# A two-block transformer kernel: position tiles as a row of the compressing layer's moving tiles, its parameters loaded during the first FFN, key zeros by VectorE, and new orders in both attentions, the FFN and the decay series

## The chip, the cores and the metric

One core of one Trainium2 chip runs the whole program. The metric is device time in microseconds (us) from the start to the end of the launch, as a median of runs. The profile is one execution of the same program.

## The reference

All is fp32 with D = 1024 features, 256 tokens and batch 1. A first block has two layers; in each, the normalized input goes through one wide projection and feeds a gated spatial unit, a latent attention with 8 heads (MLA) and a linear recurrence, whose outputs are projected, gated and merged. A second block has a pooling mixer, a convolutional FFN (FFN 0), a sparse attention (NSA) with compressed keys and values, and a second FFN (FFN 1); behind each FFN stands a gated addition ("ple"). The parts that the change touches:

```
def rg_lru(...):                      # first block, per layer
    log_a = -LRU_C * r * softplus(-lam)        # the "decay" of each of 1280 channels
    a = exp(log_a) ...
def compress(blocks, pos_emb, w1, w2):         # 15 blocks of 32 tokens, 4 groups, for keys and for values
    z = blocks + pos_emb
    z = z.reshape(z.shape[:3] + (CMP_LEN * HEAD_DIM,))
    return jax.nn.gelu(z @ w1) @ w2            # 2048 -> 128 -> 64
def conv_ffn(h, w_up, conv_w, conv_b, w_down): # 1024 -> 2 x 2816 -> 1024
def nsa_attention(...): # 16 heads; softmax over the compressed blocks, over the selected and over the windowed keys, gated
```

## The kernel before, in words

The program is raw per-engine code with semaphores; every engine's order is written out by hand. SP issues the weight loads, POOL (GpSimd) issues the small ones and does some memsets. **Weights** stream as pieces of at most 512 KB through a ring of six raw buffers (`load`): SP issues the load of a piece once PE has begun the piece five before. ACT rounds each piece to `w_hi` (L1244, `hi`), DVE computes `w_lo = raw - w_hi` (L1771, `lo`), and PE adds three products for each fp32 product (L601, L604, L605: hi by hi, lo by hi, hi by lo). In the ACT and DVE programs `hi(j, half)` and `lo(j, half)` stand where these engines make the pieces of slot j ahead, so the order of those calls among the other work decides when PE gets a piece. PSUM banks are taken in turn from two rings: J (banks 0 to 3) for projections, K (4 to 7) for side jobs.

**A norm** before a projection: ACT squares x (L1262) and takes the root (L1290), DVE the reciprocal (L1783) and a diagonal matrix (L1789), and PE multiplies x by it, which turns and scales x in one step (L724, `turn_x`, 32 matmuls, 16 for each token tile); ACT and DVE then split it into `h_hi` (L1300, `split_h`) and `h_lo` (L1805, `low_h`). Because Sqrt, Exp and the like need different tables, ACT loads a table ahead with `preload` (L1284).

**First layer's decays**: a series of 32 in-order DVE operations on 128x20 tiles (`decay_series`, `decay_terms`, `decay_result`, L1854 to L1870), placed behind `lo(0, ...)` and ahead of the convolution (L1931) in steps i = 1 to 3 of the recurrence's input projection (`l == 0` only).

**MLA**: the last gate tiles `zb` are evicted by ACT (L1249) after `hi(1, 1)`, and then come `turned` (evictions p0T, p1T of the transposed probabilities), which PE waits for at L858.

**Compressing layer**: `constant_term` (L1003 to L1009) computes w1 transposed times the position embedding as 16 matmuls of one column for the values (before `turn_x` of the ple of FFN 0) and 16 for the keys (job "bias" before `turn_x` of the key/value projection); DVE copies each to `pb` (L2348) and adds it to the hidden layer's bank. `hidden` does 2 x 16 matmuls with 60 moving columns (4 groups x 15 blocks) out of `cc`. w1 (two 1 MB loads, L576), w2, the positions and the memsets of w2 and vcz are issued by POOL in the pooling mixer's stage, just before FFN 0; POOL zeroes all of `kz` (4096 elements a partition, L580) during `turn_x` of the key/value projection.

**NSA attention**: `NSA_JOBS` is the order of the jobs on ring K: S (scores, L1097 to L1107), X (transposes of the exponentials, L1126), V (values, L1140), C (combination, L1151), "cs" (compressed scores, L1202), ct (transposes of the compressed weights Tc). ACT takes the exponentials (L1712) with the maxima that DVE makes (L2499), and evicts transposes as t0T, t1T and tcT (L1249).

## Time and profile before

| what | value |
|---|---|
| runs | 1531.07, 1532.56, 1538.85 us (median 1532.56) |
| profiled execution | 1533.47 us |
| its span in the profile | 1531.4 us |
| mean granted TensorE clock | 0.986 of full |
| DMA | 240.99 MB, mean 157 GB/s |

All times of places below are us from the start of the profiled span. A timeline row gives start, duration (of a group: from its first start to its last end), engine, line, operation, and in brackets how long the engine had been idle before and what ended that.

### The profile page before, as it was taken

The page shows a single profiled execution, that of the slowest core. Times are in us where ns is not written, and L with a number is a line of the kernel's source. Part 1 is how long each engine was busy: PE and PEld are TensorE (multiplying, and loading weights), DVE is VectorE, ACT ScalarE, POOL GpSimd, SP SyncE. Part 2 cuts the span into 40 slices and gives each one's busy share as a digit, 9 for nine tenths or more (in the row PEclk, how much of TensorE's full clock was granted, in tenths as well). Part 3 has the DMA queues.
Part 4 walks back from the last instruction along what each step waited for, and adds up shares of the span by engine and source line. Part 5 has one row for each costly group of instructions (what it writes and reads, how often), then busy time and mean ns, then how long its engine had stood idle before and what let it go on. Part 6 is the DMA issues. An engine that isn't in the chain of part 4 may idle for free.

```text
span 1531.4 us, 23284 instructions
## 1 busy us (share of the span) xinstructions
PE 1476.0 (96%) x9421; PEld 1338.5 (87%) x9421; DVE 1047.6 (68%) x1571; ACT 873.2 (57%) x1512; POOL 87.1 (6%) x137
## 2 busy tenths in 40 slices
PE   8899999999999999999999899999999989999997
PEld 7898989788789889997888799988899778999886
DVE  6645669986666366698967678864566644788745
ACT  6465756564454657565645566653674543766545
POOL 9000000007000000000000100000000000000000
PEclk9999999999999999999999999999999989999999
DMA  8524376566556144765675555556435003655553
GB/s 240 160 75 145 111 217 182 179 190 195 187 155 173 50 145 120 226 190 171 190 226 179 157 171 187 180 166 188 129 99 154 28 1 110 193 180 185 180 172 110
DMA packets 188890, 240.99 MB, mean 157 GB/s; under 512 B 19022, under 2 KB 133890, under 8 KB 188784
## 3 DMA queue, kind: packets, MB, share of 16 engines
q1 hardware_dynamic: 182944, 228.66, 49.7%
q0 software_dynamic: 5744, 10.82, 2.4%
q8 instruction: 75, 1.23, 0.3%
q14 instruction: 31, 0.25, 0.1%
q10 hardware_dynamic: 96, 0.03, 0.0%
HBM read 238.42 MB, written 1.05 MB: 156 GB/s over the span
## 4 chain that ended last, share of the span: by engine, by line
PE 84%; DVE 6%; ACT 6%; DMA 2%; issue 1%; SPq 0%; DVEq 0%; ACTq 0%
PE bank L601 24%; PE bank L605 24%; PE bank L604 24%; PE bank L724 2%; PE bank L797 2%; DVE w_lo L1771 2%; PE bank L1140 2%; ACT w_hi L1244 1%; ACT T L1712 1%; DMA raw<-in_ffn_up 1%; PE bank L1126 1%; DMA raw<-in_mla_w_ukv 1%; ACT S L1421 1%; PE bank L735 1%; DMA raw<-in_w_out 0%
## 5 line engine op out<-in xcount | busy, mean ns | idle before, releaser
L1771 DVE TENSOR_TENSOR w_lo<-raw,w_hi 128x1024 fp32r<-128x1024 f32 (+2 forms) x452 | 521.3, 1171 | 271.3 <-ACT w_hi L1244 269.1
L1244 ACT CAST w_hi<-raw 128x1024 fp32r<-128x1024 f32 (+2 forms) x452 | 450.5, 1007 | 292.6 <-DMA raw<-in_w_in 118.4
L601 PE MATMUL bank<-h_hi,w_hi 128*128 128x256 f32 (+1 forms) x1640 | 465.7, 284 | 6.2 <-issue 4.1
L604 PE MATMUL bank<-h_lo,w_hi 128*128 128x256 f32 (+1 forms) x1640 | 463.6, 283 | 0.0
L605 PE MATMUL bank<-h_hi,w_lo 128*128 128x256 f32 (+1 forms) x1640 | 463.6, 283 | 0.0
L601 PEld LDWEIGHTS bank<-h_hi,w_hi 128*128 128x128 f32 (+1 forms) x1640 | 312.9, 191 | 7.2 <-issue 7.0
L604 PEld LDWEIGHTS bank<-h_lo,w_hi 128*128 128x128 f32 (+1 forms) x1640 | 313.0, 191 | 0.1
L605 PEld LDWEIGHTS bank<-h_hi,w_lo 128*128 128x128 f32 (+1 forms) x1640 | 313.0, 191 | 0.0
L601 PE MATMUL bank<-w_hi,h_hi 128*128 128x512 f32 (+1 forms) x464 | 176.9, 381 | 1.1 <-issue 1.1
L605 PE MATMUL bank<-w_hi,h_lo 128*128 128x512 f32 (+1 forms) x464 | 175.6, 378 | 0.0
L604 PE MATMUL bank<-w_lo,h_hi 128*128 128x512 f32 (+1 forms) x464 | 175.5, 378 | 0.0
L601 PEld LDWEIGHTS bank<-w_hi,h_hi 128*128 128x128 f32 x464 | 87.3, 188 | 18.2 <-issue 2.3
L605 PEld LDWEIGHTS bank<-w_hi,h_lo 128*128 128x128 f32 x464 | 87.3, 188 | 16.5
L604 PEld LDWEIGHTS bank<-w_lo,h_hi 128*128 128x128 f32 x464 | 87.3, 188 | 15.9
L601 PE MATMUL bank<-w_hi,y_hi 128*128 128x512 f32 x176 | 69.8, 397 | 2.0 <-DVE w_lo L1771 2.0
L604 PE MATMUL bank<-w_lo,y_hi 128*128 128x512 f32 x176 | 69.6, 396 | 0.0
L605 PE MATMUL bank<-w_hi,y_lo 128*128 128x512 f32 x176 | 69.6, 395 | 0.0
L724 PE MATMUL bank<-diag,x 128*128 128x128 f32 x256 | 40.7, 331 | 10.7 <-DVE diag L1789 9.9
L724 PEld LDWEIGHTS bank<-diag,x 128*128 128x128 f32 x256 | 39.3, 243 | 12.4 <-DVE diag L1789 10.9
L1257 ACT ACTIVATE ug<-bank,par 128x256 f32<-128x256 f32 x44 | 24.9, 566 | 43.9 <-PE bank L605 43.9
L797 PE MATMUL bank<-xc,wg 128*128 128x256 f32 x208 | 45.8, 380 | 1.2 <-ACT R L1390 1.2
L797 PEld LDWEIGHTS bank<-xc,wg 128*128 128x128 f32 x208 | 39.2, 190 | 7.4 <-ACT R L1390 2.0
(356 smaller groups left out, 2150.6 us busy)
## 6 DMA issues: line engine op xcount, KB each, us to landing
raw<-in_w_in SPq DMA_DIRECT2D x160, 512.0 KB, 3.8
raw<-in_ffn_up SPq DMA_DIRECT2D x88, 512.0 KB, 3.6
raw<-in_ffn_down SPq DMA_DIRECT2D x40, 512.0 KB, 4.5
raw<-in_w_proj_a SPq DMA_DIRECT2D x16, 512.0 KB, 3.6
raw<-in_w_proj_b SPq DMA_DIRECT2D x16, 512.0 KB, 3.6
raw<-in_w_proj_c SPq DMA_DIRECT2D x16, 512.0 KB, 3.7
raw<-in_w_out SPq DMA_DIRECT2D x16, 512.0 KB, 3.7
raw<-in_ple_gate SPq DMA_DIRECT2D x16, 512.0 KB, 4.2
```

Source lines behind the costliest of these rows:

```text
L601: first = pe.matmul(out_, lh, rh, start=start, stop=False)
L604: pe.matmul(out_, lh, rl, start=False, stop=False)
L605: return pe.matmul(out_, ll, rh, start=False, stop=stop)
L724: mm = pe.matmul(ps[b][:, at:at + P], x[:, t, k * P:(k + 1) * P], diag[:, t, :], start=True, stop=True)
L735: mm = pe.transpose(ps[b][:, n * P:(n + 1) * P], src, c["ident"])
L797: mm = pe.matmul(acc(b), wg[:, g, rep, pair, :], xc[:, 5 * rep + i_, :], start=(n == 0), stop=(n == len(near) - 1))
L1126: mm = pe.transpose(ps[b][:, n * P:(n + 1) * P], src, c["ident"])
L1140: mm = pe.matmul(o_, pt, vsw[:, k, a, g * HD:(g + 1) * HD], start=k == 0, stop=k == qt)
L1244: act.copy(w_hi[b][:, 0:size], raw[b][:, 0:size]).then_inc(sems["hi_done"], 1)
L1257: act.activation(dst, acc(b), func, bias=bias, scale=scale)\
L1421: ins_ = act.activation(S[:, hd, :], S[:, hd, :], ACT.Exp, bias=sm[:, 1, col + hd:col + hd + 1], accum_out=sm[:, 2, col + hd:col + hd + 1])
L1771: dve.tensor_tensor(w_lo[b][:, 0:size], raw[b][:, 0:size], w_hi[b][:, 0:size].bitcast(F32), ALU.subtract).then_inc(sems["w_split"], 1)
```

## The change

1. `cc` gets a ninth row of 256 columns, shared by the keys' and the values' half, which holds the position embeddings at the columns that the strided view reads; the hidden layer's matmuls move 75 columns in place of 60, and both `constant_term` and their copies are gone; DVE copies the two constants out of the hidden bank with one more copy (128x2).
2. The positions and w1 are loaded in the up part of FFN 0, w1 in four quarters of 512 KB, each released by a step of it; w2 and the two memsets come behind its last step.
3. The zeros of `kz` are set by DVE, only the halves that need them, as two memsets 64x2048 in the ple of FFN 0.
4. In NSA attention the transposes of Tc go behind X1 on PE, their evictions behind t1T/t0T of head group 1 on ACT; DVE makes four `w_lo` pieces ahead of the Tc chain; ACT loads the Sqrt table behind the last t1T/t0T.
5. In both MLA layers the last zb eviction and the last `hi`/`lo` of that slot stand behind the first `turned` or the y tiles.
6. In both FFNs ACT's Sqrt table load goes from ahead of the down projection's pieces to behind those of its first half.
7. At the key/value projection ACT makes two more pieces ahead of four copies to m (`keep`).
8. The decay operations stand ahead of `lo(0, ...)`, in steps 2 to 4.
9. At the start SP issues the first weight slot before it waits for x.

```diff
-NSA_JOBS = (["bias"] + [f"norm{u}" for u in range(KT // 2)] + ["hidden", "keys0", ...]
+NSA_JOBS = ([f"norm{u}" for u in range(KT // 2)] + ["hidden", "keys0", ...]
-            + [f"X0.{i}" for i in range(6)] + ["swap3", "V0.1", "V0.0", "cs", "ct0", "ct1"]
-            + [f"X1.{i}" for i in range(6)] + ["V1.1", "V1.0", "C0"]
+            + [f"X0.{i}" for i in range(6)] + ["swap3", "V0.1", "V0.0", "cs"]
+            + [f"X1.{i}" for i in range(6)] + ["ct0", "ct1", "V1.1", "V1.0", "C0"]
...
-            sp.wait_ge(sems["x_in1"], 16)
...
                     load(0, rows_of(w_in, l, 0, KT, i * SW + COL_XC, SW))
+                    if (l, i) == (0, 0):
+                        sp.wait_ge(sems["x_in1"], 16)
...
-            pool.wait_ge(sems["sq_part"], 4 + 8 * L)
+            pool.wait_ge(sems["f_ready"], 2 + 2)
...
+            for n, key in enumerate(("cmp_w1_k_2", "cmp_w1_v_2")):
+                for half in range(2):
+                    pool.wait_ge(sems["f_ready"], 2 + 4 * (2 * n + half + 1))
+                    pool.dma_start(w1[:, n, 8 * half:8 * half + 8, :],
...
+            pool.wait_ge(sems["f_ready"], 2 + FT)
...
-            pool.wait_ge(sems["sq_part"], 4 + 8 * L + 12)
-            pool.memset(kz[:, :, :, :, :], 0.0).then_inc(sems["nsa_zero"], w.given("nsa_zero"))
...
-                if l == 0:
-                    pe.wait_ge(sems["nsa_in"], 96)
-                    filled(constant_term(side(), 1), w.bank("K"))
                 turn_x()
...
-            filled(constant_term(b, 0), b)
...
-                    mm = pe.matmul(ps[b][:, 64 * n:64 * n + 60]..., w1[:, n, k, :],
-                                   cc[:, n, :, 2 * k:2 * k + 225:16], ...)
+                    mm = pe.matmul(ps[b][:, 75 * n:75 * n + 75]..., w1[:, n, k, :],
+                                   cc[:, 4 * n:4 * n + 5, 2 * k:2 * k + 225:16], ...)
...
             scores2(2)
+            turn2(1)
             pe.wait_ge(sems["tc_done"], 1)
             for i in range(2):
                 transposes_at(job(f"ct{i}"), ...)
-            turn2(1)
...
                 if keep:
+                    keep()
...
-                        hi(j, n)
-                        evac("J", 2 * j + n, zb[:, dyn(i, 4, 2 * j + n), :], ACT.Silu)
+                        if (i, j, n) != (1, 1, 1):
+                            hi(j, n)
+                            evac("J", 2 * j + n, zb[:, dyn(i, 4, 2 * j + n), :], ACT.Silu)
...
                 turned(1, 1)
+                evac("J", -1, zb[:, HEADS - 1:HEADS, :], ACT.Silu)
...
                     y_tile(8 + n, 4 + n, yb_hi)
+                hi(-1, 1)
...
-                preload(ACT.Sqrt)
                 for n in range(2):
                     for j in range(5 if n else 6):
                         hi(j, 0), hi(j, 1)
+                    if n == 0:
+                        preload(ACT.Sqrt)
...
+            def second_slot():
+                hi(-1, 0), hi(-1, 1)
+            split_h(lambda k: col(ROW2["kv"] + k), keep=second_slot)
...
                         lo(1, 0), lo(1, 1)
+                        if l == 0:
+                            position_terms()
+                            clear_keys()
...
+            def position_terms():
+                dve.memset(cc[:, NG, :], 0.0).then_inc(sems["dve_step"], w.given("dve_step"))
+                dve.wait_ge(sems["dve_step"], w.value("dve_step"))
+                for n, key in enumerate(("posk", "posv")):
+                    dve.tensor_copy(cc[:, NG, 32 * n:32 * n + 32:2], col(ROW2[key], 16)).then_inc(sems["pos_set"], 1)
+            def clear_keys():
+                dve.memset(kz[64:P, 0, :, :, :], 0.0)
+                dve.memset(kz[0:64, 1, :, :, :], 0.0)
```

The order of DVE's instructions in the first layer's recurrence projection before, step 1 (xc is the convolution, dt the decays; ahead stand the pieces `lo(0, 0)` and `lo(0, 1)`):

```order
L1771 TENSOR_TENSOR w_lo<-raw,w_hi 128x1024 x2
L1854 TENSOR_SCALAR dt<-dt 128x20
L1855 RECIPROCAL dt<-dt 128x20
L1856 TENSOR_TENSOR dt<-dt 128x20
L1857 TENSOR_TENSOR dt<-dt 128x20
L1858 TENSOR_SCALAR dt<-dt 128x20
L1931 SCALAR_TENSOR_TENSOR xc<-bank,par,xc 128x255
```

and of the change, from the end of step 1's convolution into step 2:

```order
L1932 SCALAR_TENSOR_TENSOR xc<-bank,par,xc 128x253
L1770 TENSOR_TENSOR w_lo<-raw,w_hi 128x1024 x2
L1853 TENSOR_SCALAR dt<-dt 128x20
L1854 RECIPROCAL dt<-dt 128x20
L1855 TENSOR_TENSOR dt<-dt 128x20
L1856 TENSOR_TENSOR dt<-dt 128x20
L1857 TENSOR_SCALAR dt<-dt 128x20
L1862 TENSOR_TENSOR dt<-dt 128x20
```

The series moved from ahead of a convolution to behind the convolution and behind `lo(1, 0)` and `lo(1, 1)`; its terms follow there in the same way, four pairs or fewer a step.

DVE in the ple of FFN 0, of the change (before, the two m/x operations follow the w_lo group directly):

```order
L1804 SCALAR_TENSOR_TENSOR h_lo<-bank,par,h_hi 128x256 x8
L1770 TENSOR_TENSOR w_lo<-raw,w_hi 128x1024 x6
L2352 MEMSET cc 128x256
L2355 COPY cc<-par 128x16 x2
L2359 MEMSET kz 64x2048
L2360 MEMSET kz 64x2048
L2340 TENSOR_TENSOR m<-G,m 128x512
L2343 TENSOR_TENSOR x<-x,m 128x512
```

Five operations are added there, ahead of the additions that end in the next norm.

ACT in NSA attention, before, from the exponentials of head group 2 on:

```order
L1712 ACTIVATE T,sums<-bank,nm 128x128 x8
L1249 ACTIVATE tcT<-bank 128x512 x2
L1249 ACTIVATE t1T<-bank 128x512 x2
L1249 ACTIVATE t0T<-bank 128x512
L1724 CAST h_hi<-bank 128x512
```

and of the change:

```order
L1711 ACTIVATE T,sums<-bank,nm 128x128 x8
L1245 ACTIVATE t1T<-bank 128x512 x2
L1245 ACTIVATE t0T<-bank 128x512
L1245 ACTIVATE tcT<-bank 128x512 x2
L1723 CAST h_hi<-bank 128x512
```

The evictions of tcT moved behind those that the transposes of head group 1 fill.

## Rows read from the trace of the kernel before

**Rows 1.** The page's busy times, whole span.
```profile
PE 1476.0 (96%) x9421; PEld 1338.5 (87%) x9421; DVE 1047.6 (68%) x1571; ACT 873.2 (57%) x1512; POOL 87.1 (6%) x137
```
**Rows 2.** PE's waits: who waited for what, total us, times, longest.
```profile
PE bank L724 <- DVE diag L1789: 9.9, 4, 6.2
```
**Rows 3.** Timeline of PE, first layer, three starts of a slot.
```profile
39.13 0.36 PE L601 MATMUL bank<-h_hi,w_hi 128*128 128x256 f32 x1 [0.80 <-issue]
...
52.21 0.35 PE L601 MATMUL bank<-h_hi,w_hi 128*128 128x256 f32 x1 [1.34 <-issue]
...
65.91 0.36 PE L601 MATMUL bank<-h_hi,w_hi 128*128 128x256 f32 x1 [1.96 <-issue]
```
**Rows 4.** Timeline of DVE at the same place.
```profile
43.62 1.22 DVE L1771 TENSOR_TENSOR w_lo<-raw,w_hi 128x1024 fp32r<-128x1024 f32 x1 [2.33 <-ACT w_hi L1244]
...
48.96 0.18 DVE L1864 TENSOR_SCALAR dt<-dt 128x20 f32<-128x20 f32 x1
...
59.40 1.22 DVE L1771 TENSOR_TENSOR w_lo<-raw,w_hi 128x1024 fp32r<-128x1024 f32 x1 [3.89 <-ACT w_hi L1244]
```
**Rows 5.** Timeline of PE, MLA of the first layer.
```profile
185.81 0.46 PE L858 MATMUL bank<-p0T,vm 128*128 128x128 f32 x2 [1.38 <-ACT p1T L1249]
```
**Rows 6.** Timeline of PE, pooling mixer to FFN 0.
```profile
875.76 6.26 PE L724 MATMUL bank<-diag,x 128*128 128x128 f32 x32 [6.20 <-DVE diag L1789]
```
**Rows 7.** Timeline of DVE, same place.
```profile
871.67 1.23 DVE L1771 TENSOR_TENSOR w_lo<-raw,w_hi 128x1024 fp32r<-128x1024 f32 x1 [5.68 <-ACT w_hi L1244]
```
**Rows 8.** Timeline of ACT, same place.
```profile
870.60 1.04 ACT L1244 CAST w_hi<-raw 128x1024 fp32r<-128x1024 f32 x1 [8.71 <-DMA raw<-in_ffn_up]
```
**Rows 9.** DMA issues, 850 to 884 us: count, KB each, us to landing.
```profile
w<-in_cmp_w_v POOLq DMA_DIRECT2D x1, 1024.0 KB, 10.7
```
**Rows 10.** DMA issues, 880 to 1003 us, the up part of FFN 0.
```profile
raw<-in_ffn_up SPq DMA_DIRECT2D x39, 512.0 KB, 3.6
```
**Rows 11.** Timeline of PE, down part of FFN 0.
```profile
1018.12 0.50 PE L601 MATMUL bank<-w_hi,y_hi 128*128 128x512 f32 x1 [0.98 <-DVE w_lo L1771]
```
**Rows 12.** Timeline of ACT, same place.
```profile
1014.36 1.28 ACT L1284 ACT_TABLE_LOAD   x1
```
**Rows 13.** Timeline of PE, FFN 0 to its ple.
```profile
1071.42 3.63 PE L1007 MATMUL bank<-par,w 128*128 128x1 f32 x32
...
1080.27 0.47 PE L601 MATMUL bank<-w_hi,h_hi 128*128 128x512 f32 x1
```
**Rows 14.** Timeline of PE, FFN 1 to its ple.
```profile
1497.12 1.95 PE L724 MATMUL bank<-diag,x 128*128 128x128 f32 x16
...
1501.55 0.47 PE L601 MATMUL bank<-w_hi,h_hi 128*128 128x512 f32 x1
```
**Rows 15.** Timeline of PE, ple of FFN 0 to the key/value projection.
```profile
1102.13 3.63 PE L1007 MATMUL bank<-par,w 128*128 128x1 f32 x32
...
1113.06 0.36 PE L601 MATMUL bank<-h_hi,w_hi 128*128 128x256 f32 x1
```
**Rows 16.** Timeline of DVE, same place.
```profile
1105.49 0.16 DVE L1783 RECIPROCAL st<-st 128x1 f32<-128x1 f32 x1 [1.11 <-ACT st L1290]
```
**Rows 17.** DVE's groups by form: count, busy us, mean ns, idle before.
```profile
L2405 DVE MEMSET TcP<- 128x1024 f32 x1 | 0.9, 912 | 0.3 <-DVE sin L2402 0.3
```
**Rows 18.** Timeline of PE, key/value projection, second slot.
```profile
1120.64 0.36 PE L601 MATMUL bank<-h_hi,w_hi 128*128 128x256 f32 x1 [1.59 <-DVE w_lo L1771]
```
**Rows 19.** Timeline of PE, NSA attention.
```profile
1223.90 0.50 PE L1104 MATMUL bank<-causal_r,ident_r 128*128 128x512 f32 x1 [2.74 <-ACT T L1712]
...
1232.17 3.45 PE L1126 MATMUL bank<-cst,T 128*128 128x128 f32 x16 [3.88 <-ACT tcT L1249]
...
1254.68 0.29 PE L1140 MATMUL bank<-vsw,t1T 128*128 128x64 f32 x1 [1.31 <-ACT t1T L1249]
```
**Rows 20.** Stretches: from:to, length, busy PE, PEld, DVE, ACT, POOL, then granted clock, DMA share, GB/s.
```profile
1253.00:1264.00 11.00, 9.69 (x55) 9.48 (x54) 3.12 (x7) 2.02 (x5) 0.00 (x0) 0.65 0.01 2
...
424.00:440.00 16.00, 13.16 (x87) 11.92 (x86) 10.27 (x26) 10.14 (x27) 0.00 (x0) 1.00 0.43 126
```

More of the change, by code:

```diff
@@ L182 @@
     _at += _n
[L185 removed]
+NSA_JOBS = ([f"norm{u}" for u in range(KT // 2)] + ["hidden", "keys0", "keys1", "kc", "vc", "gates", "kc_swap", "swap0", "swap1"]
             + [f"S0.{i}" for i in range(6)] + ["swap2"] + [f"S1.{i}" for i in range(6)]
[L187 to L188 removed]
+            + [f"X0.{i}" for i in range(6)] + ["swap3", "V0.1", "V0.0", "cs"]
+            + [f"X1.{i}" for i in range(6)] + ["ct0", "ct1", "V1.1", "V1.0", "C0"]
             + [f"X2.{i}" for i in range(6)] + ["V2.1", "V2.0"] + [f"X3.{i}" for i in range(6)]
@@ L997, in ffn @@
                 w.go("J", 4)
-                if l == 0:
-                    pe.wait_ge(sems["nsa_in"], 96)
-                    filled(constant_term(side(), 1), w.bank("K"))
                 turn_x()
                 wide_square("ple", h, "h_ready", in_turn=True)
-            def constant_term(b, n):
-                for k in range(16):
-                    mm = pe.matmul(ps[b][:, n:1 + n], w1[:, n, k, :],
-                                   par[:, ROW2["posv" if n else "posk"] + k:ROW2["posv" if n else "posk"] + k + 1],
-                                   start=(k == 0), stop=(k == 15))
-                return mm
             ffn(0)
@@ L1738, in _ @@
             exps2(2)
+            turned2(1)
             for i in range(2):
                 evac("K", at(f"ct{i}"), tcT[:, 2 * i:2 * i + 2, :].rearrange("p a n -> p (a n)"), width=512)
-            turned2(1)
             high_o(0)
             exps2(3)
-            preload(ACT.Sqrt)
             high_o(1)
@@ L1747, in _ @@
             turned2(3)
+            preload(ACT.Sqrt)
             high_o(2)
@@ L1915, in _ @@
                         decay_input()
+                    if l == 0 and i == 2:
+                        decay_series()
+                        decay_terms(15, 13)
+                    if l == 0 and i == 3:
+                        decay_terms(11, 5)
+                    if l == 0 and i == 4:
+                        decay_terms(3, 1)
+                        decay_result()
                     for n in range(2):
@@ L2027, in _ @@
                         for half in range(2):
-                            lo(j, half)
+                            if (col, j, half) != (0, 1, 1):
+                                lo(j, half)
                     w.go("S", 2), w.go("J", 4)
-                for j in range(1, 5):
+                for j in range(2, 5):
                     dve.wait_ge(free[w.bank("J", -j)], w.turn("J", -j) + 1)
@@ L2048, in _ @@
                 for t in range(HEADS):
+                    if t + 1 == HEADS - 1:
+                        dve.wait_ge(free[w.bank("J", -1)], w.turn("J", -1) + 1)
                     if t + 1 < HEADS:
@@ L2562, in _ @@
             weigh2(0)
+            for j in (2, 3):
+                lo(j, 0), lo(j, 1)
             b = w.bank("K", at("cs"))
@@ L2570, in _ @@
                 .then_inc(sems["tc_ready"], 1)
-            for j in (2, 3):
-                lo(j, 0), lo(j, 1)
             w.go("S", 4), w.go("J", 8)
```

67 lines of the change are left out of this document (25 added, 42 removed).

## The prediction, made before the changed kernel was run

> **What bounds the kernel now.** I read the page first: PE is busy for 96% of the span [rows 1], so at most some 55 us are to be had from its idle time, and everything else must come from matmuls removed or from matmuls that run at a faster clock. Then I read PE's waits, in which no single cause is large; the largest is `turn_x` waiting for its diagonal, 9.9 us in four places [rows 2]. So the change can only be a collection of small holes, and I went to the timeline at each place that the diff touches. A hole counts only if the engine named before the arrow does work that the change moves, and if nothing else is ready only then.
>
> **The parts and their sum**, all against the profiled execution (1533.47 us; the median of the runs is 0.9 us lower).
>
> *Decays.* PE starts three slots late, by 0.80, 1.34 and 1.96 us [rows 3], at the steps in which DVE does 5, 8 and 11 decay operations ahead of the convolution. One takes 0.18 us and, with the wait between them, about 0.21. Moved ahead of `lo(0, 0)` they are 9, 8 and 7 operations, 1.9, 1.7 and 1.5 us. DVE stands idle there for 2.33 us in one step and 3.89 us one piece later in the next [rows 4], so they are hidden. Gain 4.1. Without that cover each would cost PE its full length again, and the gain would be 0.
>
> *MLA.* PE waits 1.38 us for the eviction of p1T [rows 5]; ahead of it on ACT stand one rounding of a piece, 1.04 us as at [rows 8], and one eviction, which leave. What is late next is the first eviction itself, so I take 1.1 for each of two layers: 2.2. The moved piece is needed only by a slot that PE reaches behind the attention, and DVE's `lo` of it follows the y tiles.
>
> *Pooling mixer to FFN 0.* DVE waits 5.68 us for a rounded piece [rows 7], because ACT waits 8.71 us for its raw load [rows 8]. At that time 2 MB of w1 are in flight, of which a megabyte took 10.7 us [rows 9]; in the up part of FFN 0 a weight piece lands 3.6 us after its issue [rows 10]. With w1 elsewhere the load is there when DVE comes, and both diagonals are ready 5.7 us earlier. PE's turn then takes 32 x 0.12 = 4 us in place of 6.26 [rows 6, 14], as its idle time shrinks from 6.2 to about 0.5 us and the clock has no reason to fall. 5.7 + 2.0 = 7.7.
>
> *Table load in the down part.* ACT loads the Sqrt table, 1.28 us [rows 12], ahead of six slots' pieces, and PE then idles 0.98 us for a `w_lo` [rows 11]. Behind the six slots ACT is ahead of PE. Two FFNs: 2.0.
>
> *First constant.* From the end of the down part to the first matmul of ple, FFN 0 takes 1080.27 - 1071.42 = 8.85 us [rows 13]; FFN 1, which has no constant, 1501.55 - 1497.12 = 4.43 us [rows 14]. Gain 4.4.
>
> *Second constant and the key zeros.* From 1102.13 to 1113.06 stand 10.93 us [rows 15]. Without the 16 columns and with DVE as now, the second diagonal, some 0.5 us behind the reciprocal at 1105.49 [rows 16], would set the end: 1106 and 2 us of turning for the second token tile, a gain of 5. But DVE gets new work ahead: a memset of 1024 elements takes 0.912 us [rows 17], so two of 2048 take up to 3.6, and with the memset of 256 and two copies 4.3. DVE has 0.5 us to spare there, so the diagonals come near 1105.0 and 1109.7, PE turns one tile, waits, turns the other and goes on at 1111.7. Gain 1.3, between 5 (all covered) and -2 (both waits at half clock).
>
> According to the Trainium skill (VectorE: DVE Perf Modes, Zero memsets can be issued as uint32 (trn2) and Specifications) a memset takes one cycle for an element at 0.96 GHz. That would be an estimate of 2.13 us for each of the two, and of 0.6 us less gain. The trace's 912 ns for 1024 elements is under the 1067 ns of that rule, and the row decides.
>
> *Position columns.* 75 columns in place of 60 cost nothing: matmuls of one column were 3.63 us for 32, 0.11 each [rows 15], which is no less than those of 128 columns [rows 14]. The copy of the constants is one small DVE operation: 0.2 against the removed two. POOL's memset of `kz` goes: 0, nobody waited.
>
> *Two pieces ahead at the key/value projection.* PE waits 1.59 us for a `w_lo` [rows 18]; the rounding comes before four copies of about half a microsecond. Gain 1.6.
>
> *NSA attention.* Three holes [rows 19]. 2.74 us: the exponentials wait for the maxima, which stand behind four `w_lo` pieces on DVE; these go into the time in which DVE waits for "cs". Gain 2.7. 3.88 us: PE's turn of X1 stands behind the transposes of Tc, whose eviction on ACT comes behind sixteen exponentials; X1 now goes first, into other banks, and about 3.0 are won, the rest being the exponentials' own. 1.31 us: the table load stands ahead of t1T: 1.3. Together 7.0.
>
> *w1 in FFN 0.* 2 MB beside a stream that lands well before it is needed: -0.3, between 0 and -4, by what the 2 MB do today in a busier place [rows 8].
>
> *Clock.* Attention runs at half clock in stretches (0.65 at 1253 to 1264), while an idle time of 3 us inside dense work shows none (1.00 at 424 to 440) [rows 20]. With holes closed but narrow matmuls packed closer I take -1, between -4 and +3.
>
> *Start.* The first slot's 1 MB is asked for ahead of x's end. PE is bound there by the small rows and x: 0, between -1 and +0.5.
>
> Sum: 4.1 + 2.2 + 7.7 + 2.0 + 4.4 + 1.3 + 1.6 + 7.0 - 0.3 - 1 = 29.0. The profiled execution would take 1504.5 us, and the median **1503.5 us**.
>
> **The rivals.**
>
> (A) *The zeros cost more than the constants gave.* The two DVE memsets make PE wait twice for about 3 us, and around two narrow, broken turns the clock stays down. The half-clock turn of [rows 6] took 6.26 in place of 4; twice that and a slower first slot are 2 to 4 us. The time would be 1506.5. For it: the stretch is narrow already. Against it: 3 us of idle did not lower the clock at 424 to 440.
> By the Trainium skill (TensorE: Matmul & The Clock Gate, What's actually happening) the slow state is the default and activity lifts it, so broken turns are punished; the trace shows both behaviours.
>
> (B) *Waits move rather than go.* In attention PE, ACT and DVE each depend on the next; a closed hole may open behind the next exponentials, and the same may hold for the decays. If half of the attention's, the decays' and the slot's gains come back, 12.7 / 2 = 6.4 are lost: 1510.
>
> (C) *w1's quarters stop FFN 0.* Each quarter may delay the weight pieces behind it. PE would have to stop for 7.3 us at each of the four to use up 29 us, as ACT did once for 8.71 [rows 8]; at the point from which this decides, 7.5 us and more each, the kernel ends slower than before, at 8.71 each 1503.5 + 34.8 = 1538. Against it: there 2 MB at once and x's norm came together, here 512 KB come over several slots, and the stream lands in 3.6 us.
> The Trainium skill (DMA: Bandwidth & Descriptors, Measured) says to batch DMAs to 1 MiB and more, which speaks against quarters; the weight pieces of half a megabyte show no such need, at 3.6 us each. A milder form, 1 to 2 us a quarter, gives 1508 to 1511.
>
> (D) *The early loads do nothing*, because something other than w1 delayed the piece at 870.6. Then 7.7 go: 1511. Against it: other pieces of the same stream land in 3.6 us.
>
> **How the numbers follow.** Forecast 0.55 (1498 to 1508), A 0.15, B 0.15, a mild C 0.06, D 0.04, strong C 0.02, and 0.03 for more gain (clock restored in attention, zeros covered, 1493 to 1498). The range of 1496 to 1512 holds the forecast, A, B and D, and leaves out strong C and the tails. 0.5% is 7.7 us, about what a measurement of this kernel can tell from no change: everything under 1524.9 counts as faster. Only a strong C or several failures at once end above: faster 0.94, same 0.04, slower 0.02.
>
> **What the profile of the changed kernel would show.** Decays: no late starts near 39, 52 and 66 us. Pooling: the wait for the diagonal falls from 6.2 to under 1.5 us, and ACT's wait for the first FFN piece is gone. Constants: no matmul of one column; ple of FFN 0 begins 4.5 us after its down part. Zeros: two waits for the diagonal of about 2.8 us each before the key/value projection. FFN 0: w1 quarters at steps 2 to 8, and no PE wait on raw pieces beside them. Attention: no wait of over 1.5 us on the maxima, tcT or t1T. It would be wrong if FFN 0 from up to down got longer by over 2 us, if the two diagonal waits together exceeded 8, or if attention shortened by less than 4.

## The result and the profile after

The changed kernel takes 1507.64 us (median of 5 runs, 1501.28 to 1510.37) against 1533.38 us for the kernel before (5 runs, 1531.07 to 1538.85): ratio 0.9826, 95% interval 0.9802 to 0.985. That is 25.7 us between the medians; 1503.5 was forecast, with 1496 to 1512 as the range. The profiled execution happened to be the shortest of the five: 1501.28 us, span 1499.5, mean clock 0.994. The other four took 1507.2 to 1510.4 at clocks of 0.990 and 0.991. So the profile shows 31.9 us of gain and the median 6 less, and what lies between them became the main question.

The busy times on the page of the changed kernel, to be read beside [rows 1]:

```profile
PE 1458.7 (97%) x9357; PEld 1321.4 (88%) x9357; DVE 1048.9 (70%) x1575; ACT 873.6 (58%) x1512; POOL 84.6 (6%) x138
```

and two of PE's waits (total, times, longest), beside [rows 2] and [rows 5]:

```profile
PE bank L730 <- DVE diag L1788: 9.4, 6, 3.8
...
PE bank L864 <- ACT p1T L1245: 0.9, 2, 0.5
```

64 matmul records are gone (9421 to 9357), the two constants. The wait for the diagonals is as large as before in sum, but it has moved: the 6.2 us ahead of FFN 0 are gone, and 3.8 and 1.1 us stand ahead of the key/value projection.

I then laid the starts of the same PE instruction in both profiles side by side. What a stage won is the change of that difference from one row to the next:

| PE instruction | before, us | after, us | difference | this stage |
|---|---|---|---|---|
| end of first turn | 13.83 | 13.71 | -0.12 | start: 0.1 |
| slot behind the last decays | 65.91 | 61.05 | -4.86 | decays: 4.7 |
| first L858 of MLA, layer 1 | 185.81 | 179.67 | -6.14 | MLA: 1.3 |
| product of c, layer 2 | 552.86 | 548.83 | -4.02 | -2.1 (scatter, below) |
| first L858 of MLA, layer 2 | 602.59 | 597.73 | -4.86 | MLA: 0.8 |
| first product of FFN 0 | 881.78 | 869.15 | -12.63 | pooling mixer: 7.8 |
| slot in its down part | 1018.12 | 1004.33 | -13.79 | w1 in FFN 0: 0; table: 1.1 |
| first product of its ple | 1080.27 | 1061.96 | -18.31 | first constant: 4.5 |
| last of the key/value turn | 1112.64 | 1093.81 | -18.83 | second constant, zeros: 0.5 |
| two slots later | 1127.11 | 1105.88 | -21.23 | pieces ahead: 2.4 |
| late in the hidden layer | 1144.83 | 1126.06 | -18.77 | given back: a wait 1.4, columns 1.1 |
| first V1 | 1235.41 | 1210.75 | -24.66 | attention: waits 4.9, clock 1.1 |
| first V2, behind the table load | 1254.68 | 1228.45 | -26.23 | table: 1.3, clock 0.3 |
| X3, behind V2 | 1267.16 | 1236.44 | -30.72 | clock in V2 and X3: 4.5 |
| slot in the down part of FFN 1 | 1443.82 | 1412.02 | -31.80 | table: 1.1 |

The rows of the changed kernel that answer to [rows 3], [rows 5], [rows 6], [rows 11], [rows 13], [rows 15] and [rows 19], PE's timeline (start, duration, instruction, idle before):

```profile
61.05 0.28 PE L607 MATMUL bank<-h_hi,w_hi 128*128 128x256 f32 x1
...
179.67 0.35 PE L864 MATMUL bank<-p0T,vm 128*128 128x128 f32 x1 [0.45 <-ACT p1T L1245]
...
865.06 1.16 PE L730 MATMUL bank<-diag,x 128*128 128x128 f32 x8 [0.43 <-DVE diag L1788]
...
1061.96 0.47 PE L607 MATMUL bank<-w_hi,h_hi 128*128 128x512 f32 x1
...
1087.73 3.40 PE L730 MATMUL bank<-diag,x 128*128 128x128 f32 x16 [3.76 <-DVE diag L1788]
1092.26 2.05 PE L730 MATMUL bank<-diag,x 128*128 128x128 f32 x16 [1.14 <-DVE diag L1788]
1094.15 0.36 PE L607 MATMUL bank<-h_hi,w_hi 128*128 128x256 f32 x1
...
1113.07 0.35 PE L607 MATMUL bank<-h_hi,w_hi 128*128 128x256 f32 x1 [1.21 <-issue]
...
1206.91 1.25 PE L1122 MATMUL bank<-cst,T 128*128 128x128 f32 x8 [0.43 <-DVE t1T L2528]
1209.85 1.07 PE L1122 MATMUL bank<-cst,TcP 128*128 128x128 f32 x8 [1.69 <-ACT t1T L1245]
1210.75 3.68 PE L1136 MATMUL bank<-vsw,t1T 128*128 128x64 f32 x32
1214.27 1.95 PE L1136 MATMUL bank<-vsw,t0T 128*128 128x64 f32 x16
```

Three things are to be seen. The late starts of the decay slots have no idle time any more. A new wait of 1.21 us stands at 1113.07, two slots behind the hole that was closed: ACT is busy without a break there, so part of what the earlier pieces gave comes back. And ahead of V1 there is a new hole of 1.69 us (1209.85): the first transpose of Tc needs a bank that ACT frees only when it evicts X1.2, behind all the exponentials of head group 2. The 4.5 us of clock are those of V2 and of the transposes behind it (X3): the kernel before ran them at half clock [rows 20], this execution at full clock. Another 1.1 us of clock lies ahead of V1: behind the hole of 3.88 us the kernel before took 3.45 us for 16 records of transposes [rows 19], and the two rows of eight here took 1.25 and 1.07. (Counts behind an x are records; a matmul of the constants or of the hidden layer leaves two.)

DVE's timeline at the zeros:

```profile
1075.76 1.76 DVE L2359 MEMSET kz<- 64x2048 f32 x1 [0.48 <-issue]
1077.99 1.76 DVE L2360 MEMSET kz<- 64x2048 f32 x1 [0.46 <-issue]
...
1087.39 0.29 DVE L1788 TENSOR_SCALAR diag<-cst,st 128x128 f32<-128x128 f32 x1
```

From the last `w_lo` of that place to the first m operation lie 5 us, and from there DVE goes on to the diagonal at 1087.4 with one break of 1.1 us, in which ACT takes the root.

### The profile page after: what moved, and what is told of

Read it like the earlier page. It is cut to its first block, busy times and chain, and to the rows that moved or that the text cites. A ratio compares the mean times of both kernels' runs of the same rounds, so it can differ in the third digit from the quotient of the medians.

```text
span 1499.5 us, 23159 instructions
## 1 busy us (share of the span) xinstructions
PE 1458.7 (97%) x9357; PEld 1321.4 (88%) x9357; DVE 1048.9 (70%) x1575; ACT 873.6 (58%) x1512; POOL 84.6 (6%) x138
## 3 DMA queue, kind: packets, MB, share of 16 engines
HBM read 238.42 MB, written 1.05 MB: 160 GB/s over the span
## 4 chain that ended last, share of the span: by engine, by line
PE 87%; DVE 6%; ACT 3%; DMA 2%; issue 2%; POOL 0%; DVEq 0%; POOLq 0%
PE bank L607 25%; PE bank L610 25%; PE bank L611 25%; PE bank L803 2%; DVE w_lo L1770 1%; PE bank L1136 1%; PE bank L730 1%; ACT T L1711 1%; PE bank L741 1%; DMA raw<-in_mla_w_ukv 1%; PE bank L1093 1%; DMA raw<-in_w_out 1%; PE bank L1050 1%; ACT w_hi L1240 1%; PE bank L1122 1%
## 5 line engine op out<-in xcount | busy, mean ns | idle before, releaser
L1599 ACT ACTIVATE sg<-ug 128x256 f32<-128x256 f32 x44 | 18.4, 418 | 46.4 <-DVE ug L2298 46.4
L730 PE MATMUL bank<-diag,x 128*128 128x128 f32 x256 | 36.0, 303 | 9.5 <-DVE diag L1788 9.4
```

Of the source, the lines that this page charges most:

```text
L730: mm = pe.matmul(ps[b][:, at:at + P], x[:, t, k * P:(k + 1) * P], diag[:, t, :], start=True, stop=True)
L1599: act.activation(sg[:, n, :], ug[:, n, :], ACT.Silu)\
```

## The experiments

**The changed kernel once more.** No edit.

> The changed kernel as it is. Its five executions so far took 1501.3 to 1510.4 us, with mean granted clocks of 0.994 (1501.3), 0.991 (1507.2, 1507.6) and 0.990 (1509.6, 1510.4). Theory 1: the difference is one or two stretches that run at half clock in most executions and at full clock in the profiled one; 0.003 to 0.004 of 1500 us are 9 to 12 us at half clock, or 4.5 to 6 us of time. Then a run of 1507 us shows such a stretch, most likely in the narrow matmuls of NSA attention (at 1228 to 1240 us in the profile of the change the clock was 1.00), and differs from the profiled one nowhere else by more than 1 us. Theory 2: the difference lies in waits on DMA spread over the program; then no single stretch holds more than half of it.

Median 1508.07 us (6 runs): 1501.1 and 1501.9 at clock 0.994, and 1508.0, 1508.1, 1508.3, 1512.5 at 0.989 to 0.991. This time the profile is of a run of 1508.02. PE's timeline of it, where the two profiles part:

```profile
1209.97 1.53 PE L1122 MATMUL bank<-cst,TcP 128*128 128x128 f32 x8 [1.69 <-ACT t1T L1245]
1211.29 6.93 PE L1136 MATMUL bank<-vsw,t1T 128*128 128x64 f32 x32
1218.01 3.62 PE L1136 MATMUL bank<-vsw,t0T 128*128 128x64 f32 x16
1221.42 1.17 PE L1144 MATMUL bank<-tcT,vcz 128*128 128x256 f32 x2
```

and the same stretch with its granted clock (third number from the end), from this profile

```profile
1211.20:1224.60 13.40, 13.40 (x63) 13.04 (x62) 2.23 (x4) 0.69 (x2) 0.00 (x0) 0.52 0.01 1
```

and from the shorter one:

```profile
1210.70:1217.50 6.80, 6.80 (x59) 6.70 (x58) 2.23 (x4) 0.95 (x2) 0.00 (x0) 1.00 0.01 2
```

The same 32 matmuls of V1 take 6.93 us in place of 3.68. Up to 1207 us no start differs by more than 0.5 us; from V1 on the difference grows by 0.1 us with each record, to 6.7 us behind the combination, and then stays. Theory 1 holds, with the place 17 us ahead of where I had put it: 1.2 GHz in one execution, 2.4 in the other, behind the same idle time of 1.69 us. The idle time two rows earlier differs a little, 0.78 us in place of 0.43.

**The old orders in NSA attention.** The three moves undone:

```diff
-            turn2(1)
             pe.wait_ge(sems["tc_done"], 1)
             for i in range(2):
                 transposes_at(job(f"ct{i}"), ...)
+            turn2(1)
...
-            turned2(1)
             for i in range(2):
                 evac("K", at(f"ct{i}"), ...)
+            turned2(1)
...
-            for j in (2, 3):
-                lo(j, 0), lo(j, 1)
             b = w.bank("K", at("cs"))
...
                 .then_inc(sems["tc_ready"], 1)
+            for j in (2, 3):
+                lo(j, 0), lo(j, 1)
...
+            preload(ACT.Sqrt)
             high_o(1)
             turned2(2)
             turned2(3)
-            preload(ACT.Sqrt)
```

> The changed kernel with the old orders in NSA attention (transposes of Tc ahead of X1, four w_lo pieces behind the Tc chain, Sqrt table ahead of t1T). If the three holes add: 2.7 + 3.0 + 1.3 = 7.0 us more, median 1514 to 1515, with waits of 2.7, 3.9 and 1.3 us at the old places. If the orders only moved waits: under 4 us more. If they also changed the clock behind them, up to 12 us more, with a half-clock stretch of some 10 us behind the transposes.

Median 1508.67 us (4 runs, 1507.93 to 1514.1): no more than the changed kernel in the same session (1508.07). The holes are all back in PE's timeline:

```profile
1205.52 0.80 PE L1100 MATMUL bank<-causal_r,ident_r 128*128 128x512 f32 x1 [4.45 <-ACT T L1711]
...
1213.80 2.02 PE L1122 MATMUL bank<-cst,T 128*128 128x128 f32 x16 [2.65 <-ACT tcT L1245]
1215.73 3.76 PE L1136 MATMUL bank<-vsw,t1T 128*128 128x64 f32 x32
...
1234.87 1.30 PE L1136 MATMUL bank<-vsw,t1T 128*128 128x64 f32 x10 [1.32 <-ACT t1T L1245]
```

Against the 1501 us profile PE is 1.9 us behind at 1190 us, ahead of the stage, and 6.4 behind at 1235 and at the end, so by place the three undone moves cost 4.6 us. (In between it was 1.5 ahead, because the scores ran at full clock in this execution; the wait of 4.45 us took that back.) V1 runs in 3.76 us here, at full clock. The fastest execution is 6.8 us above the fastest of the changed kernel in the same session (1507.93 against 1501.10), but the medians are 0.6 apart. So the new orders win 5 to 7 us against an execution without the fall of the clock, and in the typical execution the fall in V1 takes them back. That is the largest thing the change does not get. One of the four took 1514.1 at clock 0.988; no profile shows where its clock fell.

**The hole ahead of V1 closed.** ACT evicts X1.2 and X1.3 between two groups of exponentials:

```diff
-            exps2(2)
-            turned2(1)
+            exps2(2, lambda: turned2(1, (0,)))
+            turned2(1, (1,))
...
+                    if between and i == 4:
+                        between()
```

> The changed kernel, with ACT's evictions of X1.2 and X1.3 (t1T) put between the fourth and the fifth group of exponentials of head group 2, so that the banks for the transposes of Tc come free before 1208 us. If the banks are what PE waits for at 1207.9 to 1209.9 us, the hole of 1.9 us closes and V1 starts 1.5 to 1.9 us earlier. Theory K (the hole ahead of V1's narrow matmuls decides whether they run at half clock, which costs 7 us in two of three executions): with the hole closed they run at full clock in most executions, and the median falls to 1500. Rival N (the narrow matmuls of 64 columns and those ahead of them decide, whatever the hole): the same mixture of 1500 and 1506, with a median only 1.5 to 2 us lower.

Median 1501.66 us (1499.12, 1501.53, 1501.8, 1503.65), ratio to before 0.9782 (0.9766 to 0.9799). PE's timeline:

```profile
1208.80 1.25 PE L1122 MATMUL bank<-cst,T 128*128 128x128 f32 x8 [0.77 <-DVE t1T L2531]
1209.89 1.04 PE L1122 MATMUL bank<-cst,TcP 128*128 128x128 f32 x8
1210.76 2.46 PE L1136 MATMUL bank<-vsw,t1T 128*128 128x64 f32 x21
```

The hole of 1.69 us is gone, and all four executions lie within 5 us of each other at clocks of 0.994 and 0.995. The hole itself is worth 1.5 us by place; the median is about 6 lower. That difference is between sessions, since the changed kernel was not run in this one: 5 to 7 us by the ratios to the kernel before (0.9782, and 0.9826 and 0.9816 for the changed kernel, the latter with the interval 0.9788 to 0.9844, which just meets this one). Of the eleven executions of the changed kernel three were under 1503 us, of these four three and the fourth at 1503.65. Theory K holds as far as four executions can tell.

The profiles of all runs can be laid beside it. Eight have the hole of 1.7 us. From the first matmul of V1 to the job behind it they took 5.3 us in four (the changed kernel, both runs with POOL's zeros alone, w1 and w2 back), 6.1 us in one (sixty columns), and 9.3 to 10.1 us in three (the repeat, w1 as quarters, the front's parts). Four kernels have no hole there (the old orders, this run, and the two with both edits), and all four took 5.3 or 5.4 us. So the fall was seen only behind the hole, and there in half of the profiles; what decides it in a single execution stays open.

**w1 back in the pooling mixer's stage, as quarters.**

```diff
+            pool.wait_ge(sems["sq_part"], 4 + 8 * L)
+            for n, key in enumerate(("cmp_w1_k_2", "cmp_w1_v_2")):
+                for half in range(2):
+                    pool.dma_start(w1[:, n, 8 * half:8 * half + 8, :], ...)
             pool.wait_ge(sems["f_ready"], 2 + 2)
...
-                    pool.wait_ge(sems["f_ready"], 2 + 4 * (2 * n + half + 1))
```

> The changed kernel with the 2 MB of w1 asked for in the pooling mixer's stage again, as four quarters at once. If w1 delayed the raw piece there: ACT waits 8 to 9 us for it, PE 5.5 to 6.5 us for the first diagonal, and the turn behind runs partly at half clock; 7 to 8 us more, median 1515. If something else delayed that piece (rival D), no difference. FFN 0's up part loses nothing in the changed kernel, so taking the quarters out of it should gain under 0.5 us.

Median 1513.75 us (4 runs), 5.7 more than the changed kernel in the same session. Its ACT timeline, to be read beside [rows 8], and its PE timeline, beside [rows 6]:

```profile
862.13 1.04 ACT L1240 CAST w_hi<-raw 128x1024 fp32r<-128x1024 f32 x1 [3.82 <-DMA raw<-in_ffn_up]
865.17 1.05 ACT L1240 CAST w_hi<-raw 128x1024 fp32r<-128x1024 f32 x1 [1.99 <-DMA raw<-in_ffn_up]
```

```profile
870.34 3.00 PE L730 MATMUL bank<-diag,x 128*128 128x128 f32 x13 [3.40 <-DVE diag L1788]
```

The mechanism is the forecast one: ACT waits for raw pieces, DVE for ACT, PE for the diagonal (3.40 us), and the turn behind it is at half clock again. Its size is smaller than between the two kernels: FFN 0 starts 6.5 us later than in the changed kernel's profile, of which 2.3 were there before this stage, so 4.2 by place. V1 was at half clock in this execution.

**All of w1 and w2 back, in the old order**, with the two memsets ahead and w1 as two loads of 1 MB; only the positions stay in FFN 0.

> The changed kernel with w1, w2 and the two small memsets all in the pooling mixer's stage again and in the order of the kernel before, w1 as two loads of 1 MB (the positions stay in FFN 0). The quarters at once in that stage cost 3.4 us of waiting for the first diagonal and 4 to 6 us of time up to FFN 0, less than the 7.7 between the two kernels. If the rest belongs to the order (memsets and small loads first, so that w1 collides with a later piece): the wait for the diagonal is 5.5 to 6.5 us and FFN 0 starts 7 to 8 us later than in the changed kernel. If it belongs to the positions' load (128 KB, 6.6 us to landing) or to something else: as with the quarters.

Median 1511.39 us (4 runs, 1506.58 to 1515.05). Its ACT timeline and its PE timeline:

```profile
863.43 1.04 ACT L1235 CAST w_hi<-raw 128x1024 fp32r<-128x1024 f32 x1 [6.00 <-DMA raw<-in_ffn_up]
```

```profile
868.59 6.48 PE L725 MATMUL bank<-diag,x 128*128 128x128 f32 x32 [3.48 <-DVE diag L1783]
874.83 0.36 PE L602 MATMUL bank<-h_hi,w_hi 128*128 128x256 f32 x1
```

FFN 0 starts 874.83 - 869.15 = 5.7 us later than in the changed kernel. Of this 0.5 was there before the stage, and 2.1 are the turn at half clock (6.48 us for 32 records). That makes 5.3 by place, and the order of the loads does not explain the missing 2.5 us of the 7.8; whether the positions' 128 KB do (their load took 6.6 us to land in the kernel before), or the chance by which w1 and a raw piece meet, stays open.

**POOL's zeros, released early.**

```diff
+            pool.wait_ge(sems["sq_part"], 4 + 8 * L + 8)
+            pool.memset(kz[:, :, :, :, :], 0.0).then_inc(sems["nsa_zero"], w.given("nsa_zero"))
...
-                            clear_keys()
...
+            dve.wait_ge(sems["nsa_zero"], 2)
```

> The changed kernel with the zeros of kz set by POOL again (one memset, 3.5 us), but released already by the end of FFN 0's down part, so that DVE has no such work. Theory A (DVE's two memsets of 1.76 us made PE wait 3.9 and 1.4 us for the two diagonals ahead of the key/value projection): the first diagonal comes about 3.9 us earlier, the waits become about 0.3 and 2.5 us, and PE begins the projection 3 to 4 us earlier; the median is 3 to 4 us lower, 1504. Theory B (the root and table loads on ACT set the diagonals anyway): the waits stay within 1 us of 5.3 in sum, and the median stays at 1507.

Median 1504.57 us (6 runs, 1501.31 to 1508.99). PE no longer waits for the first diagonal of the key/value projection (3.76 us before) and comes 3.9 us nearer there, as theory A has it, but it has lost 4.3 us at 1060, ahead of and in the ple. From FFN 0 to the key/value projection the edit gains 0.2 us in this profile. So the median, 3.5 us under the changed kernel's in the same session and close to the 1504 of theory A, does not bear that theory out: three of these six executions ran at clock 0.994 and two of the changed kernel's six, and the ranges overlap almost wholly. POOL's and DVE's timelines there:

```profile
1060.41 3.51 POOL L588 MEMSET kz<- 128x4096 f32 x1 [51.80 <-ACT G L1260]
```

```profile
1060.91 3.09 DVE L1790 TENSOR_SCALAR diag<-cst,st 128x128 f32<-128x128 f32 x1
```

The diagonal, 0.29 us elsewhere, took 3.09 and ended with POOL's memset. The timelines of POOL and DVE in the kernel before have the same pair of rows:

```profile
1105.19 3.51 POOL L580 MEMSET kz<- 128x4096 f32 x1 [245.80 <-ACT G L1262]
```

```profile
1105.69 3.09 DVE L1789 TENSOR_SCALAR diag<-cst,st 128x128 f32<-128x128 f32 x1
1105.89 2.89 DVE L2348 COPY pb<-bank 128x1 f32<-128x1 f32 x1
```

The last row is the copy of the second constant, one element a partition out of PSUM; it stood behind the diagonal and ended with it, and PE, which was busy with the first turn, waited 0.8 us for the two.

**POOL's zeros beside operations that read PSUM.** As the last one, but with

```diff
-            pool.wait_ge(sems["sq_part"], 4 + 8 * L + 8)
+            pool.wait_ge(sems["h_hi_done"], 8 * (L + 2) + 1)
```

> POOL's zeros once more, but released by the first h_hi of the ple of FFN 0, beside operations of DVE that read a PSUM bank. Theory P (a POOL memset holds up a DVE operation whose operands all lie in SBUF: the diagonal took 3.09 us in place of 0.29 beside it, in the kernel before and with the earlier release alike): here the h_lo operations keep their 0.48 us, no diagonal is late at 1060 us, and PE reaches the key/value projection 3 to 4 us earlier than in the changed kernel. Rival (every DVE operation beside it is held up): the h_lo chain is 3 us longer, and the gain is 0 to 1 us.

Median 1504.67 us (4 runs). POOL's timeline and DVE's:

```profile
1062.88 3.54 POOL L588 MEMSET kz<- 128x4096 f32 x1 [53.92 <-ACT h_hi L1298]
```

```profile
1061.25 0.29 DVE L1790 TENSOR_SCALAR diag<-cst,st 128x128 f32<-128x128 f32 x1
1062.85 3.39 DVE L1806 SCALAR_TENSOR_TENSOR h_lo<-bank,par,h_hi 128x256 fp32r<-128x256 f32 x8 [1.31 <-ACT h_hi L1298]
```

The eight h_lo operations take 3.39 us beside the memset, as they do in the changed kernel without it (3.39 at 868.52), and the diagonal is back at 0.29. From the last matmul ahead of the turn to the first of the key/value projection PE takes 6.0 us, where the changed kernel takes 10.6 and the kernel before 11.2; the forecast had 3 to 4 us less, it is 4.5. Four executions: 1498.3, 1503.8, 1505.6 and 1511.3, at clocks of 0.995, 0.992, 0.991 and 0.986. The scatter of the changed kernel is still there, and so is the hole ahead of V1.

Theory P says more than this shows. At the start every kernel has DVE operations with both inputs in SBUF beside a longer memset of POOL. POOL's timeline and DVE's in the kernel before:

```profile
13.73 5.68 POOL L543 MEMSET wg<- 128x6656 f32 x1
```

```profile
15.53 1.21 DVE L1771 TENSOR_TENSOR w_lo<-raw,w_hi 128x1024 fp32r<-128x1024 f32 x1
```

The `w_lo` operation takes the 1.22 us that it takes elsewhere. So it is not enough that all operands lie in SBUF; what was stopped has one tensor as its source.

**Both edits together.**

> Both edits together: POOL's zeros beside the h_lo operations, and the evictions between the exponentials. If both theories hold, 3.5 + 1.8 us less and mostly full clock in V1: median 1497. If only the sizes hold and the clock goes on falling in two of three executions: 1503.

Median 1495.41 us (1493.47, 1495.36, 1495.47, 1496.27), ratio to before 0.9741 (0.9726 to 0.9755). This is 9.3 us less than with POOL's zeros alone and 6.3 less than with the hole closed alone, in one session. By place the zeros are worth 2.5 us in this profile, in which the second turn ran at half clock, and 4.5 with the zeros alone, and the hole 1.5. V1 stays at 2.4 GHz, and so did the stretch ahead of it (granted clock third from the end),

```profile
1185.00:1200.00 15.00, 13.04 (x84) 10.51 (x83) 13.05 (x21) 3.69 (x11) 0.00 (x0) 1.00 0.00 0
```

which in the changed kernel's profile was partly at half clock:

```profile
1189.00:1200.00 11.00, 11.00 (x63) 8.93 (x62) 9.29 (x12) 1.42 (x2) 0.00 (x0) 0.73 0.00 0
```

The second stretch is worth little, though. The scores took 3.5 us in place of 5.8, and then PE waited for the exponentials of head group 2, as its waits show:

```profile
PE bank L1102 <- ACT T L1715: 2.0, 1, 2.0
```

so that about 1 us of it is left. Why the stretch recovered was not taken apart. Of the 6.1 us between this profile and that of the closed hole alone, 3.3 were there at 1083 us already, ahead of both edits, where the two kernels are the same; most of them came between 430 and 560 us. So the steps between these medians say less than the places do. The interval of the ratio lies clear of the changed kernel's (0.9788 to 0.9844 in the repeat), so the kernel with both edits beats the one before and the changed one.

**Two of four w_lo pieces later.**

```diff
-            for j in (2, 3):
-                lo(j, 0), lo(j, 1)
+            lo(2, 0), lo(2, 1)
             b = w.bank("K", at("cs"))
...
             weights2(1)
+            lo(-1, 0), lo(-1, 1)
             weigh2(1)
```

> Both edits of best2, and in NSA attention DVE makes only two of the four w_lo pieces ahead of the Tc chain and the other two behind turned2(1), where it waits some 5 us for V1. In best2's profile PE waits 1.96 us for the exponentials of head group 2, because the four pieces end at 1193.6 us, while the scores are there. If that hole is a plain wait on DVE, it closes and the median falls by about 2 us to 1493.5. If ACT or V1's banks come next, under 1 us. If the clock in V1 depends on what lies ahead, the scatter of 7 us comes back.

Median 1495.87 us (6 runs, 1494.34 to 1498.89), ratio 0.9764 (0.9737 to 0.979), which overlaps with the last one. In its profile the wait of 1.96 us for the exponentials is gone (PE goes from one job to the next at 1197.26), and PE gains 2.1 us there on the other profile. But it had come there 1.9 us later, by late starts ahead of 52 us and a turn at 430 us that fell to half clock in this execution. So the hole closed, and the medians, which are from two sessions, do not show it: inconclusive.

**The front's three parts undone together**: the decays, the zb piece and the Sqrt table as in the kernel before.

> The changed kernel with three parts undone that lie in different stages: the decay operations behind lo(0, .) again, the last zb piece ahead of the turned tiles in both MLA layers, and the Sqrt table ahead of the down pieces in both FFNs. If each is worth what the two traces show: PE starts late by 1.0, 1.5 and 2.1 us at 38, 51 and 64 us; by 1.0 us more in each MLA layer; by 1.1 us in each FFN. Together 8.8 us of span, each at its own place and nowhere else. If the stages give some of it back later (waits that move), less than 7.

One execution, 1515.93 us. The starts against the changed kernel's profile: later by 1.05, 1.56 and 2.19 us at 39, 52 and 66 us (decays 4.8), by 1.14 at 1010 and by 1.13 at 1426 (tables). PE's waits of it:

```profile
PE bank L864 <- ACT p1T L1245: 2.8, 2, 1.4
```

That is 1.9 us more than the changed kernel's 0.9. The three parts add up to 4.8 + 1.9 + 2.3 = 9.0 us by place, against 8.8 expected. The whole is 14.4 us, because V1 fell to half clock in this execution, too (its first 32 records took 6.11 us; from 1214 to 1232 us PE lost 6.6).

**Sixty columns in the hidden layer.**

```diff
-   mm = pe.matmul(ps[b][:, 75 * n:75 * n + 75]..., w1[:, n, k, :], cc[:, 4 * n:4 * n + 5, ...], ...)
+   mm = pe.matmul(ps[b][:, 90 * n:90 * n + 60]..., w1[:, n, k, :], cc[:, 5 * n:5 * n + 4, ...], ...)
```

> The changed kernel with 60 moving columns in the hidden layer's matmuls: it leaves the position terms out of the compressed keys and values (the constants are read from two columns of the hidden bank). In the traces the 64 matmul records take 0.11 us apart with 60 columns and 0.13 with 75. If that is the price of the fifteen columns, the hidden layer is 1.2 us shorter, and nothing else moves by more than 0.5 us. If the prediction's view holds (columns under 128 are free), no difference.

One execution, 1503.13 us. PE's timeline:

```profile
1120.35 7.28 PE L1050 MATMUL bank<-cc,w 128*128 128x60 f32 x64
```

PE's timeline of the changed kernel has

```profile
1118.89 8.52 PE L1050 MATMUL bank<-cc,w 128*128 128x75 f32 x64
```

The position columns cost 1.24 us. The prediction had 0. Elsewhere starts moved by up to 3 us, as they do from one execution to the next, so the rest of the expectation can't be judged on one execution.

## Why the prediction was right or wrong

The time lies in the range, 4.1 us above the forecast. Most terms are right by mechanism and by size. By place, what is missing are a stretch that no part touches (-2.1), the position columns (-1.2), the attention's new hole (-0.8), the zeros (-0.8) and the pieces at the key/value projection (-0.6); the decays, w1 and others gave 1.6 more than forecast. By steps, with the forecast gain in brackets:

*Decays* (4.1): 4.7 by the two profiles, 4.8 by the undoing. Right; I had summed the idle times, and each slot start was lost by 0.15 to 0.2 more than its idle time says. (The part that moved is 24 operations, 5 + 8 + 11, and not the 32 of the section on the kernel before.) *MLA* (2.2): 2.1 between the profiles, 1.9 by the waits. Right. *Table in the down parts* (2.0): 2.2, and 2.3 by the undoing. Right. *First constant* (4.4): 4.5. Right. *w1 in FFN 0* (-0.3): 0. In the up part the weight pieces landed in 4.4 us in place of 3.6 [rows 10], and PE waited for none. Strong C is refuted, and so is a mild C.

*Pooling mixer* (7.7): 7.8 between the profiles. The mechanism is shown by both undoings, which brought the wait on the raw piece, the wait for the diagonal and the half-clock turn back; only 4.2 and 5.3 us of the size came back with them. D is refuted.

*Second constant and zeros* (1.3): 0.5. The waits of about 2.8 and 2.8 us came as 3.8 and 1.1. What was mis-sized is DVE's new work: the five operations took 5.0 us (1074.72 to 1079.68, with half a microsecond ahead of each memset) where the forecast had 4.3, and both diagonals came about 1 us later than it had them. A wrong statement beside it did not hurt the sum: the removal of POOL's memset was put at nothing because "nobody waited". The diagonal took 3.09 us beside that memset and PE waited 0.8 us for it, so the old way of zeroing had a price. It is contained in the measured 1113.06 from which the gain was counted. The early POOL zeros showed it by moving the 3.09 us to another diagonal. The later ones avoided both prices, and with them the stretch is 5.1 us shorter than in the kernel before, as the upper bound of 5 (all covered) had it.

*Two pieces ahead* (1.6): 2.4 at their place, of which 1.4 came back two slots later as a wait at 1113.07: B in small. *Position columns* (0): -1.2, a term that was put at nothing. The reason was the cadence of matmuls in other lines: 0.11 us a record for one column [rows 15], which is in fact less than the 0.12 of those with 128 columns [rows 14]. Those cadences do not carry over: 75 columns of the hidden layer's strided view take 0.13, more than 128 columns of a turn. Whether the columns or the fifth group of the view cost the 0.02 was not separated.

*Attention* (7.0): the three holes gave 2.7 + 3.5 + 1.3 = 7.5 by their idle times, but the new order made one of 1.7, which leaves 6.2 between the profiles (4.9 + 1.3); the undoing has 4.6 by place. Right for the holes that were there; the new one was not foreseen, and with it fails the sign that no wait on maxima, tcT or t1T would be over 1.5 us. The transposes of Tc behind X1 wait for a bank that ACT frees late. This is B again, at the one place where it was dear: a hole of 1.7 us, and behind it 6.7 us of lost clock in the typical execution.

*Clock* (-1, between -4 and +3): in the profiled execution it was +5.9, of which 4.5 in V2 and X3, outside the bounds; in the typical one, by the repeat, 6.7 less, which is -0.8 and close to the forecast. That it came out close is luck: it is the difference of a gain in V2, which the forecast had only as a chance of 0.03, and of a loss in V1, which it did not have. The mechanism that was given (narrow matmuls packed closer) is not what the runs show. V1 fell only behind a hole and stayed at full clock in the four profiles in which it follows without one.

*A*: the waits for the diagonals were there, and the profiled execution shows the second turn at full clock and the first at half; the term came out 0.8 us under the forecast, not 3.

The stretch from 431 to 553 us, where 2.1 us were lost, is touched by no part of the change. PE idles 2.84 us there for a diagonal in every profile; behind it the turn took 2.05 us in the kernel before and 3.17 in the changed kernel, and with the matmuls behind it 1.5 us of the 2.1 are explained. Of the thirteen profiles the turn ran at full clock in three (the kernel before, the front's parts undone, and the first kernel with both edits) and wholly or mostly at half clock in ten. My argument that 3 us of idle do not lower the clock [rows 20] rested on one throw. PE's timeline of the changed kernel there:

```profile
428.69 3.17 PE L730 MATMUL bank<-diag,x 128*128 128x128 f32 x16 [2.84 <-DVE diag L1788]
```

## What to carry to other kernels

A hole in front of a run of narrow matmuls costs more than its length: here, behind 1.7 us of waiting, 6.7 us were lost to half clock in some executions and not in others, and without the wait in no profile. If several executions of a kernel scatter in two groups, profile it twice and lay the starts of the same instructions side by side; the place shows at once. When an order is changed, look at which engine frees the PSUM bank of the moved job, and not only at its operands. And before an operation of one engine is costed at nothing because nobody waits for it by name, look at whether its neighbours run longer beside it. A median that lands on a forecast is no proof of it when the executions scatter by more than the gain: read the gain at its place.

## What the runs showed of the hardware

A POOL memset of 128x4096 fp32 (3.51 us) stopped a DVE operation with one source tensor in SBUF (the 128x128 fp32 diagonal, 0.29 us alone) until it ended: 3.09 us, at two places of two kernels. DVE operations that read PSUM and one SBUF tile (h_lo) kept their time beside it: 3.39 us for eight, with and without. So did one with two source tensors in SBUF beside a memset of 128x6656: w_lo, 1.21 us. The Trainium skill (GPSIMD Engine Reference, Specifications) says that POOL shares its SBUF interfaces with VectorE, with contention where DVE runs in a two-port mode or has two SBUF inputs, and another page of the Trainium skill (VectorE: DVE Perf Modes, Mode 2×_2P) that an fp32 operation with a single SBUF source and a constant is such a two-port case and one on PSUM is not. The rows of the diagonal and of h_lo agree with both. The row of w_lo does not agree with the part on two SBUF inputs, and the measurement decides for this memset.

The same idle time of PE was followed by 2.4 GHz in some executions and by 1.2 GHz in others: 2.84 us at 430 (three profiles and ten), 1.7 us at 1210 (four, one in part, and three). A DVE memset of 64x2048 fp32 took 1.76 us, 0.86 ns an element; [rows 17] scaled up gave 1.82. The Trainium skill's one cycle an element (VectorE: DVE Perf Modes, Zero memsets can be issued as uint32 (trn2)) would be, by an estimate at its 0.96 GHz (Specifications), 2.13 us; the trace does not agree, and the measurement decides. Records of matmuls with 60 fp32 columns of a strided view started 0.11 us apart, those with 75 columns 0.13.
